# Key-selection scores of a sparse-attention layer: weighting and summing over the heads, moved from ScalarE and GpSimd to TensorE

## What is computed

```python
iqh = iq.reshape(Bsz, T, 8, 64) * 64 ** -0.5
iwh = iw * 8 ** -0.5
rel = relu(einsum('bqhd,bsd->bqhs', iq_b, ik))        # per head h: queries x keys
score = einsum('bqh,bqhs->bqs', iw_b, rel)            # weight per query and head, sum over 8 heads
score = where(visible, score, -inf)                   # causal
_, idx = top_k(score, 128)
```

## Time and profile before

| | |
|---|---|
| median of the runs | 4105.53 us |
| the profiled execution's own time | 4110.7 us |
| its span | 4108.9 us |
| PE / DVE / ACT / POOL busy | 91% / 52% / 34% / 2% of the span |
| mean granted TensorE clock | 0.936 of full |
| prepare stage, layer 0 and layer 1 | about 2143 to 2209 us and 3371 to 3444 us |

### The profile page before, as it was taken

How to read it: one execution, slowest core, us unless ns; L and a number is a source line. 1 busy time by engine, 2 the same in 40 slices (tenths; PEclk the granted TensorE clock), 3 DMA queues, 4 the chain that set the end, 5 groups by cost and what they waited for, 6 DMA issues and landing times. The chain is left out here.

```text
span 4108.9 us, 60704 instructions
## 1 busy us (share of the span) xinstructions
PE 3727.7 (91%) x25912; PEld 3210.0 (78%) x25912; DVE 2139.9 (52%) x3354; ACT 1379.3 (34%) x2129; POOL 93.8 (2%) x99
## 2 busy tenths in 40 slices
PE   7878999699889997999998679999999998679998
PEld 6878999588789996888875448888888875548886
DVE  6666663444356644443346765444443357765443
ACT  3324332345433323322215243323222215243321
POOL 0000000000000000000003000000000003000000
PEclk9989999899889998999997789999999997789999
DMA  3212333121123331333310013333233310013332
GB/s 125 63 49 82 93 87 92 56 67 59 47 63 97 92 90 58 104 96 95 101 56 2 6 58 98 98 93 100 96 96 98 98 50 2 6 53 97 98 92 77
DMA packets 86413, 306.95 MB, mean 75 GB/s; under 512 B 9585, under 2 KB 9713, under 8 KB 85761
## 3 DMA queue, kind: packets, MB, share of 16 engines
q1 hardware_dynamic: 86144, 303.08, 23.6%
HBM read 300.91 MB, written 2.13 MB: 74 GB/s over the span
## 5 line engine op out<-in xcount | busy, mean ns | idle before, releaser
L572 DVE TENSOR_TENSOR two_w_lo<-two_raw,two_w_hi 128x1024 fp32r<-128x1024 f32 (+1 forms) x344 | 412.9, 1201 | 847.3 <-ACT two_w_hi L563 844.3
L587 PE MATMUL psum<-two_x_hi,two_w_hi 128*128 128x512 f32 x1856 | 725.9, 391 | 28.5 <-DVE two_w_lo L572 28.5
L587 PE MATMUL psum<-two_x_lo,two_w_hi 128*128 128x512 f32 x1856 | 723.2, 390 | 0.0
L587 PE MATMUL psum<-two_x_hi,two_w_lo 128*128 128x512 f32 x1856 | 723.1, 390 | 0.0
L563 ACT CAST two_w_hi<-two_raw 128x1024 fp32r<-128x1024 f32 (+1 forms) x344 | 352.6, 1026 | 897.3 <-PE psum L587 892.9
L587 PEld LDWEIGHTS psum<-two_x_hi,two_w_hi 128*128 128x128 f32 x1856 | 349.1, 188 | 103.2 <-DVE two_w_lo L572 29.2
L1360 PE MATMUL psum<-one_x_hi,one_w_hi 128*128 128x264 f32 x1408 | 402.5, 286 | 23.1 <-DVE one_x_lo L1504 21.1
L587 PEld LDWEIGHTS psum<-two_x_lo,two_w_hi 128*128 128x128 f32 x1856 | 349.1, 188 | 73.8 <-issue 1.4
L587 PEld LDWEIGHTS psum<-two_x_hi,two_w_lo 128*128 128x128 f32 x1856 | 349.1, 188 | 72.5
L1360 PE MATMUL psum<-one_x_lo,one_w_hi 128*128 128x264 f32 x1408 | 401.4, 285 | 0.0
L1360 PE MATMUL psum<-one_x_hi,one_w_lo 128*128 128x264 f32 x1408 | 401.1, 285 | 0.0
(11 more groups left out here) (403 smaller groups left out, 6588.5 us busy)
## 6 DMA issues: line engine op xcount, KB each, us to landing
two_raw<-in_swi_in SPq DMA_DIRECT2D x176, 512.0 KB, 3.6
one_raw<-in_ffn_in SPq DMA_DIRECT2D x88, 512.0 KB, 3.6
two_raw<-in_swi_out SPq DMA_DIRECT2D x64, 448.0 KB, 3.3
two_raw<-in_mix_in SPq DMA_DIRECT2D x56, 512.0 KB, 3.6
one_raw<-in_attn_w SPq DMA_DIRECT2D x32, 512.0 KB, 3.9
two_raw<-in_swi_out SPq DMA_DIRECT2D x32, 512.0 KB, 3.5
one_raw<-in_ffn_out SPq DMA_DIRECT2D x32, 448.0 KB, 3.3
one_raw<-in_lru_w SPq DMA_DIRECT2D x24, 512.0 KB, 3.6
```

The costliest lines, as they stand in the source:

```text
L572: self.nc.vector.tensor_tensor(self.m.ws.lo[:, u % self.SLOTS, w], self.m.raw[:, u % self.RAW, w], self.m.ws.hi[:, u % self.SLOTS, w].bitc ...
L587: last = self.nc.tensor.matmul(self.m.ps[:, bank, :], a[:, u % self.SLOTS, w], b[:, k0 + k, :], start=(start and k == 0 and q == 0), stop= ...
```

## The change

Each unit's weight column is put on a 128 x 128 diagonal: ScalarE copies the identity with the column as scale (ring of four buffers). PE multiplies relu(unit) by that diagonal, in fp32, and adds up the eight heads of a block in PSUM bank 4 (`total`, two units behind `score`). ScalarE copies the finished sum to the block's score (`keep`); GpSimd only masks. ScalarE's second pass over the unit and GpSimd's copy and additions are gone. Since bank 4 is taken, the bonus products use banks 3, 5, 3, and the third waits until VectorE has read the first.

```diff
--- before.py
+++ after.py
@@ -1669,10 +1669,12 @@
     early = ((0, 2), (2, 6), (6, 10))
     NT = SEQ // P
     inverse = w.norm
+    diagonal = [m.work[:, 4 + j, 0:P] for j in range(4)]
     col = lambda n, c: m.col(f"rwkv_{n}{layer}", c)
     with stage(nc, f"rwkv_prep{layer}", "loaded", "lo_ready", "mv_ready", "z_psum", "z_out", "cum_ready", "exp_out", "sq_ready",
                "ss_psum", "ss_ready", "root_ready", "spread", "prod_ready", "bonus_psum", "bonus_out", "v_saved", "own",
-               "scaled", "iw_psum", "iw_ready", "rel_psum", "rel_out", "relu_ready", "relu_used", "hidden") as (block, s):
+               "scaled", "iw_psum", "iw_ready", "rel_psum", "rel_out", "diagonal", "rel_used", "summed", "sum_out",
+               "hidden") as (block, s):
         @block.sync
         def _(sp):
             sp.dma_start(w.lo_w, d["rwkv_lo"][layer]).then_inc(s["loaded"], 16)
@@ -1688,6 +1690,19 @@
                     pe.wait_ge(s["rel_out"], u - 1)
                 nc.tensor.matmul(m.ps[:, 6 + h % 2, 0:n], m.other[half(h), 4 + h // 2, b * QB:n],
                                  m.other[half(h), 8, 0:n], start=True, stop=True).then_inc(s["rel_psum"], 1)
+
+            def total(u):
+                i, h = heads[u]
+                n = (blocks[i] + 1) * QB
+                if h == 0 and i:
+                    pe.wait_ge(s["sum_out"], i)
+                pe.wait_ge(s["rel_out"], u + 1)
+                pe.wait_ge(s["diagonal"], u + 1)
+                last = nc.tensor.matmul(m.ps[:, 4, 0:n], diagonal[u % 4], ix.relu[u % 4][:, 0:n], start=(h == 0),
+                                        stop=(h == IH - 1)).then_inc(s["rel_used"], 1)
+                if h == IH - 1:
+                    pe.wait_ge(s["rel_used"], u + 1)
+                    pe.sem_inc(s["summed"], 1)
 
             for n in range(SEQ // P):
                 last = nc.tensor.transpose(m.ps[:, 6, n * 8:(n + 1) * 8], m.other[0:8, 15, n * P:(n + 1) * P],
@@ -1719,6 +1734,8 @@
                     last.then_inc(s["ss_psum"], 1)
                 for u in range(*early[c]):
                     score(u)
+                    if u >= 2:
+                        total(u - 2)
             pe.wait_ge(s["z_out"], C)
             pe.wait_ge(s["root_ready"], 1)
             for c in range(C):
@@ -1731,10 +1748,15 @@
                 last.then_inc(s["spread"], 1)
             for c in range(C):
                 pe.wait_ge(s["prod_ready"], c + 1)
-                nc.tensor.matmul(m.ps[:, 3 + c, :], m.head_ones, w.prod[c], start=True, stop=True).then_inc(
+                if c == 2:
+                    pe.wait_ge(s["bonus_out"], 1)
+                nc.tensor.matmul(m.ps[:, 3 + 2 * (c % 2), :], m.head_ones, w.prod[c], start=True, stop=True).then_inc(
                     s["bonus_psum"], 1)
             for u in range(early[-1][1], len(heads)):
                 score(u)
+                total(u - 2)
+            for u in (-2, -1):
+                total(len(heads) + u)
 
         @block.scalar
         def _(act):
@@ -1743,14 +1765,19 @@
             def weigh(u):
                 i, h = heads[u]
                 b = blocks[i]
-                rel = ix.relu[h % 4][:, 0:(b + 1) * QB]
+                if u >= 4:
+                    act.wait_ge(s["rel_used"], u - 3)
+                nc.scalar.activation(diagonal[u % 4], m.ident[:, :], ACT.Copy,
+                                     scale=ix.iw[:, b * IH + h:b * IH + h + 1]).then_inc(s["diagonal"], 1)
                 act.wait_ge(s["rel_psum"], u + 1)
-                if u >= 4:
-                    act.wait_ge(s["relu_used"], u - 3)
-                nc.scalar.activation(rel, m.ps[:, 6 + h % 2, 0:(b + 1) * QB], ACT.Relu).then_inc(s["rel_out"], 1)
-                act.wait_ge(s["rel_out"], u + 1)
-                nc.scalar.activation(rel, rel, ACT.Copy, scale=ix.iw[:, b * IH + h:b * IH + h + 1]).then_inc(
-                    s["relu_ready"], 1)
+                nc.scalar.activation(ix.relu[u % 4][:, 0:(b + 1) * QB], m.ps[:, 6 + h % 2, 0:(b + 1) * QB],
+                                     ACT.Relu).then_inc(s["rel_out"], 1)
+                if u >= 2 and heads[u - 2][1] == IH - 1:
+                    keep(i - 1)
+
+            def keep(i):
+                act.wait_ge(s["summed"], i + 1)
+                nc.scalar.copy(ix.score[blocks[i]], m.ps[:, 4, 0:(blocks[i] + 1) * QB]).then_inc(s["sum_out"], 1)
 
             for c in range(C):
                 act.wait_ge(s["z_psum"], c + 1)
@@ -1772,6 +1799,7 @@
                 nc.scalar.activation(w.el[:, c, :], w.cum[:, c, :], ACT.Exp).then_inc(s["exp_out"], 1)
             for u in range(early[-1][1], len(heads)):
                 weigh(u)
+            keep(2)
 
         @block.gpsimd
         def _(pool):
@@ -1779,16 +1807,7 @@
                 nc.gpsimd.tensor_copy(m.v_first[:, :, :], w.v).then_inc(s["v_saved"], 1)
             for i, b in enumerate(blocks):
                 score = ix.score[b]
-                for h in range(IH):
-                    u = IH * i + h
-                    rel = ix.relu[h % 4][:, 0:(b + 1) * QB]
-                    pool.wait_ge(s["relu_ready"], u + 1)
-                    if h == 0:
-                        nc.gpsimd.tensor_copy(score, rel).then_inc(s["relu_used"], 1)
-                    else:
-                        pool.wait_ge(s["relu_used"], u)
-                        nc.gpsimd.tensor_tensor(score, score, rel, ALU.add).then_inc(s["relu_used"], 1)
-                pool.wait_ge(s["relu_used"], IH * (i + 1))
+                pool.wait_ge(s["sum_out"], i + 1)
                 diag = score[:, b * QB:(b + 1) * QB]
                 nc.gpsimd.affine_select(out=diag, in_=diag, compare_op=ALU.is_ge, fill=HIDDEN, base=0,
                                         pattern=[[-1, QB]], channel_multiplier=1).then_inc(s["hidden"], 1)
@@ -1855,7 +1874,8 @@
                 nc.vector.tensor_tensor(k, k, neg, ALU.mult).then_inc(s["scaled"], 1)
                 nc.vector.tensor_tensor(r, r, w.el[:, c, :], ALU.mult).then_inc(s["scaled"], 1)
                 dve.wait_ge(s["bonus_psum"], c + 1)
-                own.then(nc.vector.tensor_tensor(w.bonus[:, c, :], m.ps[:, 3 + c, :], w.v[:, c, :], ALU.mult))
+                nc.vector.tensor_tensor(w.bonus[:, c, :], m.ps[:, 3 + 2 * (c % 2), :], w.v[:, c, :], ALU.mult).then_inc(
+                    s["bonus_out"], 1)
 
 
 def rwkv_recurrence_stage(nc, m, layer):
```

## The result

The changed kernel takes **4134.33 us** (median, 4132.88 to 4135.68), the kernel before 4108.07 in the same comparison: a ratio of 1.0064, interval 1.0047 to 1.0081. That is 26.3 us slower; 4136 was predicted, 30.7 slower. The ratios of this document leave out executions in a slow state: one of the run "pairs, one pass" took 4798.6 us, and its median of 4096.2 counts it, while that of its other six is 4095.4.

What follows compares the result with a forecast made beforehand. PE was taken to bound the early part, ScalarE the tail. Layer 1's +15.9 and layer 0's +14.8 us gave +30.7: 4141.4 on the profiled 4110.7, 4136 on the median 4105.5; range 4118 to 4152.

Steps and rivals of the forecast that it cites:

- Early part: Ahead of the spread: added totals and scores no longer side by side, +8.1 us in layer 1, +7.0 in layer 0.
- Bonus: Third bonus product waits for VectorE's read of the first bank: +0.1 us a layer, at most 1.
- Tail: Last part of the stage: PE becomes the bound at full clock, 30.3 us against 22.0, +8.3 a layer.
- Next stage: Its start may find full clock because PE idles less before it: 0 to -1.3 us, -0.6 a layer taken.
- Loads: Weight loads between scores and totals: all hidden, -10 us a layer, 4116; totals' loads costing twice, +5 a layer, 4146.
- Pace of the old tail: In the tail before the change ScalarE sets the pace: 2.76 us from one relu to the second next, 1.38 a unit.
- The early rise of the clock: Rival: full clock comes in the middle of group 1, leaving about +6.5 us a layer, 4118; chance 0.08.
- The lower level in the tail: Rival: the tail runs at clock 0.50, +24 us a layer, 4161 with one layer, 4185 with both; chance 0.08.
- The rival on the faster side: In the tail, removing ScalarE's and POOL's path wins if score plus total take PE under 1.38 us: 4095; chance 0.03.

Runs made afterwards that it cites:

- pairs, one pass: Changed kernel with scores and totals ordered in twos, block 1's sum copied behind the exponentials, relu and diagonal held as fp32r: 4096.2 us, ratio 0.9969.
- filled run: Kernel before with 18 idle identity products on PE behind its last score: 4104.9 us, ratio 0.9993.
- pairs: Changed kernel with PE's order in twos (score, score, total, total): 4101.4 us, ratio 0.9987 to the kernel before.
- the paired order and the late copy: Changed kernel with PE's order in twos and ScalarE copying block 1's sum behind its exponentials instead of ahead of the root: 4099.2 us, ratio 0.9979.

## Why the prediction was right

The early parts and the tails, which make nearly all of the sum, came as they were priced and for the reason given: PE's serial time in those places. The one large miss is a small term, the next stage. Two errors ran against each other, but by 0.7 and 1.3 us only, so the total isn't luck.

- **Early part.** Predicted 9.0 and 9.9 for layer 1's two groups; measured 9.20 (3406.97 to 3416.17) and 10.05 (3422.18 to the last total's 3431.08 + 1.15). A total of 256 columns at the lower clock was taken as 1.10 and is 1.15. The spread came 8.5 and 7.3 us later, predicted 8.1 and 7.0. Leaving the totals out gives it back, so this is shown. The lost pairing and the copy ahead of the root are in it: the copy began 0.13 behind the last total and took 0.37, predicted 0.15 and 0.38.
- **Bonus.** PE waited 0.39 in layer 0; in layer 1 the third product began at 3441.23, 0.1 behind the end of VectorE's read (3440.43 + 0.69). The three products took 0.6 and 0.3 longer than before, predicted 0.1 each; the spread ahead of them, at a higher mean clock (0.62 and 0.56 instead of 0.58 and 0.50), took 0.3 and 0.5 less, which wasn't predicted.
- **Tail.** Predicted costs of 0.85, 1.06, 0.84 and 1.05; measured 0.84, 1.06, 0.84 and 1.06. The clock stayed at 1.00, as in the alternation of the earlier trace rows. The tail grew by 7.6 in layer 0 and 7.7 in layer 1 (30.6 against 23.0 and 22.9, to the next stage), predicted 8.3. The end is cheaper by its last three totals, which take 2.84 together as back-to-back products do.
- **Next stage.** This term was mis-sized: predicted -0.6 a layer with -1.3 as the end of its bounds; measured -2.1 and -2.5. No row stood behind the -1.3. The gain is the transposes': at full clock three take 0.33 instead of 0.64, so eight threes take 2.5 less; from them to the first masked product it is 2.2 at all times. The filled run of the kernel before shows that the clock alone does this. That the opening finds the clock up isn't assured by PE's shorter idle time, though: with pairs, PE stood idle 2.07 us before both openings, as in the changed kernel, and behind equal tails layer 1's took 4.9 and layer 0's 6.5 (0.50 from 2206.4 on). This term makes 3.3 of the 4.4 us by which the forecast was too high; the tails make 1.3, spread and bonus 0.2, and the early parts came 0.7 dearer. The last 0.3 is between profiles and medians.
- **Loads.** Neither bound was touched. A lone total costs 1.05 and a second one behind it 0.86, so the loads of the first are in the open and those of the second hide; the rule of the Trainium skill (TensorE: Matmul & The Clock Gate, Part 3, The mechanism), by which loads hide only behind products in other rows, is contradicted by this second total.
- **Pace of the old tail.** The prediction says that ScalarE set it. ScalarE was busy for about 2.5 of the 2.76 us, but each relu of 512 columns that waited did so for PE (0.17 in the earlier trace rows), and the score that it waited for had started when the relu before it left the bank (3431.77 + 0.60) and passed at the lower clock:

```profile
3432.42 3.31 PE L1689 MATMUL psum<-two_other 64*128 64x512 f32 x4
```

So the 2.76 are one relu, 0.60, one score at the lower clock, 2.07 (3432.42 to 3434.49, the first of the two in this row), and the handovers. It changes no term, since 1.38 a unit was measured and not derived.
- **Range.** The prediction's lower bound of the sum, 4116, lies outside its range, and of the upper end, 4152, only 4150 is accounted for (4146 and 4). Neither mattered.
- **Rivals.** The early rise of the clock didn't come in the changed kernel, in either layer, and did in the paired order. The lower level in the tail didn't come. The rival on the faster side priced ScalarE's and GpSimd's path; the additions alone are worth 2.6 to 3.2 a layer. It was right that PE's time per unit decides: at 1.49 a unit (pairs) the tail was even with before.

## What to carry to other kernels

Before moving work to TensorE, cost it in the place where it lands: here two half-height products had shared the array, and one full-height product between them cost its own time and theirs. Order such products in twos, halves together and full ones together, which was worth 33 us here without removing an operation. And where a product only applies a diagonal, ask how many passes its type takes: of what it replaced here, GpSimd's additions were hidden but for about 3 us a layer.

## What the runs showed of the hardware that was not expected

- Products of fp32 with 64 rows are paced the same as those with 128 when alone: 0.84 and 0.84 us at 384 columns, 1.06 and 1.06 at 512, both at full clock, and 1.15 and 1.15 at 256 at the lower level. Half the rows saved nothing.
- Useless work on PE raised the clock for useful work: with 18 products of the identity by itself in an idle stretch, the next stage's transposes passed at 0.33 us a group of three (3450.62 to 3450.94) instead of 0.64.
- One alternation of 64-row scores and 128-row totals stood at either level of the clock in the same execution: at 0.50 in 3407:3416 (busy 9.00 of 9.00 us, 256 columns) and at 1.00 in 3442.3:3468 (25.55 of 25.70, 384 and 512 columns), where it followed the spread and the bonus.
- With the paired order and the late copy, four passes went with an early clock rise in layer 1 (1.00 from 3391 on) and one pass didn't (0.50 in 3377:3406), so that the spread came 3.5 us later with less work on PE. That one pass is the cause isn't shown: each is one profiled execution, and pairs alone, with four passes, stayed at 0.50 in layer 1 too.
